# A second pair of projection tiles by Strassen's method in 5 of 11 iterations of a feed-forward layer

## The reference

```
h = x @ w_up + b_up                      # 512 x 1024 times 1024 x 5632
h = causal_depthwise_conv(h, w_dw, b_dw) # width 3
g, val = split(h)                        # 2816 channels each
y = (silu(g) * val) @ w_down + b_down
x = layer_norm(alpha * x + y)
```

## Time and profile before

| | before |
|---|---|
| median of 3 runs | 1030.0 us |
| span of the profiled execution | 1027.8 us |
| what lies around the span, taken against the median | 2.2 us |
| DVE, ACT, POOL busy, share of the span | 78%, 49%, 22% |
| mean granted clock of TensorE | 0.998 of full |

### The profile page before, as it was taken

The page is one execution under the profiler, slowest core; times in us unless marked ns, Lnnn a source line. Parts: engine busy times, 40 slices in busy tenths (PEclk is TensorE's granted clock), DMA queues, the critical chain, the costliest instruction groups (busy, mean ns, idle before and its releaser), DMA issues.

```text
span 1027.8 us, 14241 instructions
## 1 busy us (share of the span) xinstructions
PE 1016.9 (99%) x4731; PEld 842.4 (82%) x4731; DVE 806.6 (78%) x1156; ACT 504.1 (49%) x739; POOL 224.6 (22%) x279
## 2 busy tenths in 40 slices
PE   9999999999999999999999999999999999999997
PEld 7777787988888888888888888898888888888885
DVE  6999978687767767787895869768777776778888
ACT  6889864333334334465454443344343343346553
POOL 1998730413440000000010200052334000000001
PEclk9999999999999999999999999999999999999999
DMA  9756269899995232376655333879999523228652
GB/s 335 217 159 164 62 151 347 177 265 290 228 259 143 102 102 82 118 271 204 195 175 201 118 111 112 308 154 284 270 235 248 148 82 105 99 88 264 201 197 111
DMA packets 64428, 189.71 MB, mean 185 GB/s; under 512 B 7424, under 2 KB 8448, under 8 KB 63872
## 3 DMA queue, kind: packets, MB, share of 16 engines
q1 hardware_dynamic: 44144, 137.76, 39.4%
q0 software_dynamic: 18224, 44.05, 21.7%
q10 hardware_dynamic: 2016, 7.34, 2.0%
HBM read 178.11 MB, written 54.53 MB: 226 GB/s over the span
## 4 chain that ended last, share of the span: by engine, by line
PE 84%; DVE 3%; issue 1%; DMA 1%; ACT 1%; POOL 0%; DVEq 0%; POOLq 0%; ACTq 0%
PE ps L1671 17%; PE ps L1669 17%; PE ps L1670 17%; PE ps L1908 6%; PE ps L1907 6%; PE ps L1906 6%; PE ps L1679 4%; PE ps L1681 4%; PE ps L1680 4%; PE ps L1836 1%; DMA raw<-d_weights 1%; DVE ps L1173 1%; PE ps L1951 1%; PE ps L1953 1%; PE ps L1952 1%
## 5 line engine op out<-in xcount | busy, mean ns | idle before, releaser
L1669 PE MATMUL ps<-xh,wh 128*128 128x512 f32 x816 | 320.3, 392 | 0.4 <-DVE wl L1077 0.3
L1671 PE MATMUL ps<-xh,wl 128*128 128x512 f32 x816 | 317.6, 389 | 0.0
L1670 PE MATMUL ps<-xl,wh 128*128 128x512 f32 x816 | 317.5, 389 | 0.0
L1669 PEld LDWEIGHTS ps<-xh,wh 128*128 128x128 f32 x816 | 153.2, 188 | 33.6 <-issue 1.2
L1670 PEld LDWEIGHTS ps<-xl,wh 128*128 128x128 f32 x816 | 153.2, 188 | 32.8 <-issue 1.2
L1671 PEld LDWEIGHTS ps<-xh,wl 128*128 128x128 f32 x816 | 153.2, 188 | 32.1
L687 ACT ACTIVATE wh<-raw 128x1024 fp32r<-128x1024 f32 x114 | 119.9, 1056 | 81.4 <-PE ps L1908 63.3
L1077 DVE TENSOR_TENSOR wl<-raw,wh 128x1024 fp32r<-128x1024 f32 x101 | 122.6, 1220 | 41.7 <-ACT wh L687 39.9
L536 POOL TENSOR_SCALAR veps<-sqs 128x1 f32<-128x1 f32 x15 | 4.8, 323 | 561.5 <-ACT squares L881 561.5
L1402 DVE TENSOR_TENSOR wl<-raw,wh 128x1024 fp32r<-128x1024 f32 x80 | 97.6, 1220 | 7.6 <-ACT wh L935 7.6
L1906 PE MATMUL ps<-wh,parts 128*128 128x512 f32 x264 | 102.7, 389 | 0.0
(11 more groups left out here) (199 smaller groups left out, 1657.7 us busy)
## 6 DMA issues: line engine op xcount, KB each, us to landing
raw<-d_weights SPq DMA_DIRECT2D x156, 512.0 KB, 4.0
raw<-summed SPq DMA_DIRECT2D x56, 512.0 KB, 4.1
summed<-d_weights POOLq DMA_DIRECT2D x88, 256.0 KB, 8.1
summed<-d_weights SPq DMA_DIRECT2D x66, 256.0 KB, 7.5
summed<-summed POOLq DMA_DIRECT2D x46, 256.0 KB, 5.0
wl<-raw POOLq DMA_DIRECT2D x4, 1024.0 KB, 7.2
wl<-raw POOLq DMA_DIRECT2D x5, 512.0 KB, 7.3
xraw<-d_x_fm SPq DMA_DIRECT2D x8, 256.0 KB, 6.1
```

Source lines behind the costliest of these rows:

```text
L1669: eng.matmul(ps[:, bank, cols], a, xh[:, k, cols], start=(k == 0), stop=False)
L1670: eng.matmul(ps[:, bank, cols], a, xl[:, k, cols], start=False, stop=False)
L1671: mm = eng.matmul(ps[:, bank, cols], b, xh[:, k, cols], start=False, stop=(k == KD - 1))
```

## The change

Iterations 2 to 6 of 11 treat their second tile (units c = 2 and 3) otherwise. The 256 x 1024 weights (gate and value, each as two halves of 4 blocks) and x (two halves of channels, two halves of 256 positions) are taken as 2 x 2 blocks, and the product is made of 7 products of 12 matmuls with 256 columns in place of 8 blocks' worth (48 matmuls of 512 columns).

- The four sums of x are made once per layer by POOL (`x_sums`, 10 operations of 1024 elements per partition), ahead of its DMA steps. ACT and DVE split them (`t_h`, `t_l`, 4 of 1024 each) between iterations 1 and 2.
- The four sums of weights are made per iteration by POOL in the raw buffers (`w_sums`, 4 operations of 512 elements), once the low part of v2 is made. Between them POOL issues its DMA steps: 5 before the first set, 8 behind each.
- ACT and DVE split the sums; DVE adds bias, product and a copy that ACT took of the PSUM bank (`kept`, `block`, 256 columns each, 4 an iteration).
- SP loads into the raw buffers of such a pair only after the low parts of the sums.
- In all iterations the first tap is done by ACT, a second pass over the bank with the tap's weight as scale and a bias that POOL computes once (`tapb`); DVE does two taps.
- PE waits, ahead of a unit, for ACT's reads (`g_in`, `v_in`) in place of the first tap.
- Buffers for the early units, the norm's scratch and one wait (unit U_UP1 - 1, now for the last spatial product) are moved to make room.

The diff, cut to its core:

```diff
+S_FROM, S_TO = 2, 7
+NS = S_TO - S_FROM
+T_ROWS = slice(S_TO, S_TO + 4)
+POOL_STEPS = [5, 8, 8, 8, 8, 8]
...
         elif u == BEFORE_EARLY[1]:
-            eng.wait_ge(v_n, NT)
+            eng.wait_ge(sp, GROUPS)
...
         for u in range(2 * RAW, UNITS):
             eng.wait_ge(*lo_of(u - RAW))
+            if strassen_pair(u - RAW):
+                m, c = strassen_pair(u - RAW)
+                eng.wait_ge(s_lo, 3 * m + (3 if c == 2 else 2))
...
+        eng.tensor_tensor(tapb[:, :], par[:, C_FUP_B:C_FUP_B + n], newest, ALU.mult).then_inc(tapb_ok, 1)
+        eng.wait_ge(tapb_ok, 1)
+        eng.tensor_tensor(tapb[:, :], tapb[:, :], par[:, C_FDW_B:C_FDW_B + n], ALU.add).then_inc(tapb_ok, 1)
...
+        def x_sums(layer):
+
+            eng.wait_ge(x_lo, XN[2 * layer])
...
+            eng.tensor_tensor(t_f[0], b12[0], b11[0], ALU.subtract).then_inc(t_sum, 1)
+            eng.tensor_tensor(t_part[0], b12[1], b11[1], ALU.subtract).then_inc(t_sum, 1)
+            eng.wait_ge(t_sum, n + 2)
+            eng.tensor_tensor(t_f[0], t_f[0], t_part[0], ALU.add).then_inc(t_sum, 1)
...
+        def w_sums(layer, m):
...
+            eng.wait_ge(*lo_of(u + 1))
+            eng.tensor_tensor(a22, a21, a22, ALU.add).then_inc(s_sum, 1)
+            eng.wait_ge(s_sum, n + 1)
+            eng.tensor_tensor(a21, a11, a21, ALU.subtract).then_inc(s_sum, 1)
+            eng.wait_ge(s_sum, n + 2)
+            eng.tensor_tensor(a11, a22, a11, ALU.subtract).then_inc(s_sum, 1)
+            eng.wait_ge(s_sum, n + 3)
+            eng.tensor_tensor(a12, a12, a11, ALU.subtract).then_inc(s_sum, 1)
+
+        def up_sums(layer):
+
+            x_sums(layer)
+            done = POOL_STEPS[0]
+            summed_weights(layer, 0, done)
+            for m in range(NS):
+                w_sums(layer, m)
+                summed_weights(layer, done, done + POOL_STEPS[m + 1])
+                done += POOL_STEPS[m + 1]
+            summed_weights(layer, done, 5 * KQ)
```

ScalarE, the Strassen iteration and the order of the iterations:

```diff
+            def started(i, q, v):
...
+                eng.activation(buf[:, FPAD:], bank, ACT.Identity, bias=par[:, bass.ds(column(i, q, v) + C_FUP_B, 1)])
+                if v == 0:
+                    products_read(i, q)
+                eng.activation(acc[:, :], bank, ACT.Identity, scale=par[:, bass.ds(newest_at(i, q, v), 1)],
+                               bias=tapb[:, bass.ds(column(i, q, v), 1)]).then_inc(signal, 1)
...
+            def strassen(i):
+
+                eng.wait_ge(w_used, i * 4 + u0)
+                eng.wait_ge(raw_in[raw3], i * 16 + loads_of(raw3) + 16 * ((u0 + 3) // RAW))
+                eng.activation(v2h[:, :], raw[:, raw3, HALF:UNIT], ACT.Copy).then_inc(w_hi, 1)
+                started(i, 0, 0)
+                ahead(i, 1)
+                eng.wait_ge(s_sum, i * 4 + (4 * m0 + 2))
+                eng.activation(wh[:, three, :], raw[:, raw3, :], ACT.Copy).then_inc(s_hi, 1)
+                eng.wait_ge(s_sum, i * 4 + (4 * m0 + 3))
+                eng.activation(sum2h[:, :], raw[:, raw2, 0:HALF], ACT.Copy).then_inc(s_hi, 1)
+                started(i, 0, 1)
+                eng.wait_ge(st_pe, i * 5 + (5 * m0 + 1))
+                kept(i, 0, 0, x_bank)
+                eng.wait_ge(s_sum, i * 4 + (4 * m0 + 4))
+                eng.activation(wh[:, two, 0:HALF], raw[:, raw2, HALF:UNIT], ACT.Copy).then_inc(s_hi, 1)
+                gate(i, 0)
+                ahead(i, 2)
+                eng.wait_ge(st_pe, i * 5 + (5 * m0 + 3))
+                kept(i, 1, 1, y_bank)
+                high(i, 0)
+                eng.wait_ge(st_pe, i * 5 + (5 * m0 + 4))
+                kept(i, 0, 1, x_bank)
+                eng.wait_ge(st_pe, i * 5 + (5 * m0 + 5))
+                kept(i, 1, 0, z_second)
+                ahead(i, 3)
+                products_read(i, 1)
...
+                gate(i, 1)
+                high(i, 1)
+
+            regular(0, lambda c: his([u0 + c + LEAD] if c else []))
+            with eng.Fori(1, S_FROM) as i:
+                regular(i, lambda c: ahead(i, c))
+            for j in (0, 1, 3, 2):
+                eng.wait_ge(t_sum, T_SUMS * layer + T_ENDS[j])
+                eng.activation(t_h[j], t_f[j], ACT.Copy).then_inc(t_hi, 1)
+            eng.wait_ge(res_ok, NT * (2 * layer + 1))
+            with eng.Fori(S_FROM, S_TO) as i:
+                strassen(i)
+            with eng.Fori(S_TO, KQ) as i:
+                regular(i, lambda c: ahead(i, c))
```

VectorE:

```diff
+            def strassen(i):
+
+                eng.wait_ge(w_hi, i * 4 + (u0 + 4))
+                eng.tensor_tensor(v2l[:, :], raw[:, raw3, HALF:UNIT], v2h[:, :].bitcast(f32), ALU.subtract).then_inc(w_lo, 1)
+                taps(i, 0, 0)
+                ahead(i, 1)
+                eng.wait_ge(s_hi, i * 3 + (3 * m0 + 1))
+                eng.tensor_tensor(wl[:, three, :], raw[:, raw3, :], wh[:, three, :].bitcast(f32), ALU.subtract).then_inc(s_lo, 1)
+                eng.wait_ge(s_hi, i * 3 + (3 * m0 + 2))
+                eng.tensor_tensor(sum2l[:, :], raw[:, raw2, 0:HALF], sum2h[:, :].bitcast(f32), ALU.subtract).then_inc(s_lo, 1)
+                taps(i, 0, 1)
+                eng.wait_ge(s_hi, i * 3 + (3 * m0 + 3))
+                eng.tensor_tensor(wl[:, two, 0:HALF], raw[:, raw2, HALF:UNIT], wh[:, two, 0:HALF].bitcast(f32), ALU.subtract).then_inc(s_lo, 1)
+                hidden(i, 0)
+                ahead(i, 2)
...
+                block(i, 0, 0, z_first)
...
+                block(i, 0, 1, y_bank)
+                ahead(i, 3)
...
+                block(i, 1, 1, x_bank)
+                block(i, 1, 0, x_bank)
+                taps(i, 1, 0)
+                taps(i, 1, 1)
+                hidden(i, 1)
...
+            for n, j in enumerate((0, 1, 3, 2)):
+                eng.wait_ge(t_hi, 4 * layer + n + 1)
+                eng.tensor_tensor(t_l[j], t_f[j], t_h[j].bitcast(f32), ALU.subtract).then_inc(t_lo, 1)
+            with eng.Fori(S_FROM, S_TO) as i:
+                strassen(i)
```

TensorE:

```diff
+            def strassen_units(i):
+
+                eng.wait_ge(w_lo, i * 4 + (u_up + 3 - len(BY_DMA)))
+                eng.wait_ge(v_in, i * 2 + KH * layer)
+                part(x_bank, wh[:, two, first], wl[:, two, first], b11, True).then_inc(st_pe, 1)
+                part(z_first, wh[:, two, second], wl[:, two, second], b21, True).then_inc(st_pe, 1)
+                eng.wait_ge(s_lo, i * 3 + (3 * m0 + 1))
+                part(y_bank, wh[:, three, second], wl[:, three, second], b_t[0], True).then_inc(st_pe, 1)
+                eng.wait_ge(s_lo, i * 3 + (3 * m0 + 2))
+                eng.wait_ge(snap, i * 4 + (4 * m0 + 1))
+                part(x_bank, sum2h, sum2l, b_t[1], False).then_inc(st_pe, 1)
+                eng.wait_ge(w_lo, i * 4 + (u_up + 4 - len(BY_DMA)))
+                part(z_second, v2h, v2l, b_t[3], True).then_inc(st_pe, 1)
+                eng.wait_ge(s_lo, i * 3 + (3 * m0 + 3))
+                eng.wait_ge(snap, i * 4 + (4 * m0 + 2))
+                part(y_bank, wh[:, two, first], wl[:, two, first], b22, False).then_inc(w_used, 1)
+                eng.wait_ge(snap, i * 4 + (4 * m0 + 3))
+                part(x_bank, wh[:, three, first], wl[:, three, first], b_t[2], False).then_inc(w_used, 1)
+
+            with eng.Fori(1, S_FROM) as i:
                 for c in range(4):
...
+                    regular_unit(i, c)
+            eng.wait_ge(t_lo, 4 * (layer + 1))
+            with eng.Fori(S_FROM, S_TO) as i:
+                for c in range(2):
+                    regular_unit(i, c)
+                strassen_units(i)
+            with eng.Fori(S_TO, KQ) as i:
+                for c in range(4):
+                    regular_unit(i, c)
```

More of the change, by code:

```diff
@@ L630, in issue @@
                     eng.dma_start(out, of).then_inc(w_sum[i % AHEAD], 16)
[L632 removed]
+            for step in range(first_step, last_step):
+                phase, i = divmod(step, KQ)
                 turn(i)
[L634 to L639 removed]
@@ new lines, in ffn_up, with ahead @@
+            other = 4 - bank0
+            x_bank, y_bank = ps[:, bank0 + 3, 0:HQ], ps[:, bank0 + 2, 0:HQ]
+            z_second = ps[:, other + 1, 0:HQ]
+            two, three = [(slot0 + c) % RING for c in (2, 3)]
+            raw2, raw3 = [(u0 + c) % RAW for c in (2, 3)]
+            m0 = layer * NS - S_FROM
+            pads = ((gpad, gacc, g_in), (vpad, vacc, v_in))
+            def ahead(i, c):
+                slot, part = (slot0 + c + LEAD) % RING, (u0 + c + LEAD) % RAW
+                eng.wait_ge(w_used, i * 4 + (u0 + c + LEAD - RING + 1))
+                eng.wait_ge(raw_in[part], i * 16 + loads_of(part) + 16 * ((u0 + c + LEAD) // RAW))
+                eng.activation(wh[:, slot, :], raw[:, part, :], ACT.Copy).then_inc(w_hi, 1)
@@ L930, in ffn_up, with regular @@
[L930 to L937 removed]
+            def regular(i, split):
+                for q in range(2):
+                    split(2 * q)
+                    started(i, q, 0)
+                    split(2 * q + 1)
+                    started(i, q, 1)
+                    gate(i, q)
```

(1 more changed line is left out.)

292 lines of the change are left out of this document (193 added, 99 removed).

## The result

The changed kernel takes 1123.9 us (median of 4 runs, 1122.0 to 1125.5) against 1030.3 for the kernel before in the same session: ratio 1.0917, 95% interval 1.0903 to 1.0930. The forecast was 1113, range 1065 to 1145. The profiled execution, the shortest of the four (1122.0), has a span of 1120.2, 92.4 more than the 1027.8 of before.

The account below looks back on a forecast made before the run. It took TensorE, busy 99% of a 1027.8 us span, as the bound. Per layer -4.0 + 25.5 + 2 + 18.2 = +41.7; two layers +83.4; 1027.8 + 83.4 + 2.2 = 1113 us, range 1065 to 1145.

Parts of the forecast that it names:

- the three places it named: PE idle in iteration 1 (late low weight part), before iteration 2 (11 us), and at product 3 of iterations 3 to 6.
- Term 1: Strassen's products on PE: 84 matmuls of 256 columns replace 48 of 512, saving 0.80 us a pair, 8.0 in all.
- Term 2: PE's wait for the splits of the input sums, in iteration 1 and before iteration 2: 25.5 us lost per layer.
- 197.7 + 37.2 + 20: Time of the input sums' last low part: first taps' start, VectorE's work, eight remaining GpSimd sums; together 254.9 us.
- The floor of 10.8: Least idle PE per layer before iteration 2, 10.8 us, from splitting the input sums if nothing else is late.
- Term 3: PE's clock falls when idle; restart at half speed after the 11 us wait costs 2 us per layer, between 0 and 4.
- The second rival: More than counted: half-clock matmuls after each 4.4 us wait, late GpSimd DMA steps; 1135 to 1160, chance 0.12 above 1145.
- Term 4: PE waits inside Strassen iterations for low parts of weight sums: 3.2 us in the second, 5.0 in three others, 18.2 per layer.
- Edits at nothing: GpSimd's DMA steps, ScalarE's first tap, the later unit wait cost nothing; the small tap-bias operations at most 1.5 us once.
- They just fit: GpSimd's eight DMA steps, 21 us, plus 5.6 of sums fit the about 28 us between first and second sets of sums.
- POOL's sums run beside DVE: GpSimd's sums overlap VectorE or find its gaps: 1060, half exclusion some 1085; chance 0.22 for 1055 to 1085.
- Faster: PE's wait for input-sum splits passes during earlier matmuls, weight sums' low parts come by 13.8: 1022 us, chance 0.02.

Follow-up runs that it names:

- e11: Changed kernel with Strassen in iterations 3 to 6 only, all sums by VectorE, splits reordered, PE's wait inside, product 5 before 3 and 4: 1030.2 us, ratio 1.0016.
- e3: Changed kernel with the ten sums of inputs moved from GpSimd to VectorE, behind its last low part of x: 1108.6 us.
- e4: Changed kernel with GpSimd's DMA steps per iteration 11, 0, 8, 8, 9, 9 instead of 5, 8, 8, 8, 8, 8: 1115.3 us.
- e2: Changed kernel without Strassen: all iterations regular, no sums, first tap still on ScalarE: 1029.4 us against 1029.5 for the kernel before, ratio 0.9997.
- e8: Changed kernel with PE's wait inside, splits earlier, sums of inputs by VectorE, and the sums of weights by VectorE too: 1057.7 us.

## Why the prediction held, and where it didn't

The direction and the main mechanism held: the forecast's own case (1085 to 1145) came true, with PE idle at the three places it named. The sum, 1113, is 10.9 under the measured 1123.9, and two errors of opposite sign are in it: idle 87.4 forecast, 77.0 measured (-10.4); clock 4 forecast, 23.1 measured (+19). That it came within 1% is partly luck. (The two errors make 9 of the 10.9; the profiled execution took 1122.0.)

- **Term 1, products, -8.0**: held (20.92 us an iteration in e11). The gap of the Trainium skill, by which it would have been 11.9, did not; the section gives that formula for a matmul by itself and not for a stream with weight loads, as this one is.
- **Term 2, 25.5 of idle a layer**: 19.1 (7.33 + 11.75). The step that failed is the sum "197.7 + 37.2 + 20": it put GpSimd's time and VectorE's end to end, as if each operation kept the other engine out for its whole length. VectorE did wait like that, but GpSimd's ten sums took 27.0 for 24.4, so of VectorE's 6.5 us of own work in that stretch only 2.6 came on top and 3.9 lay inside GpSimd's. That is the size of the miss: by the prediction's own numbers iteration 2 starts 254.9 - 229.2 = 25.7 late (it says 25.5), and it started some 21.5 late, of which 19.1 is idle and 2.5 the slow matmuls behind the first wait. The floor of 10.8 was close (11.75, and 12.9 in e3, where nothing of GpSimd's stood in the way).
- **Term 3, clock, +2 a layer**: some 12 (23.1 in the two). This is the most mis-sized term. It counted one restart a layer; there are five, since the wait in iteration 1 and those inside the iterations are followed by a lower clock too. The size of one restart, 1.4 to 2.7, is close to the 2 assumed. (The 18 transposes at the start stand 0.213 apart, not 0.228, and the same shape stands 0.108 apart later, at full clock, so the reading as the low level is borne out.) The second rival had this price ("each wait of 4.4 us costs half-clock matmuls", 1.3 to 2 us in six iterations); it belonged in the sum.
- **Term 4, 18.2 a layer**: 20.1 and 18.5, so the number held and its working did only in part. It gave 3.2 and three times 5.0; measured were 7.6, 2.6, 6.5, 3.4. The chain alone makes product 3 wait 2.5 (e4, iteration 3), where the forecast had 4.4 at product 3 and 5.0 in all. In that iteration v2's low part was done 8.2 us behind the previous iteration's last product, for the 10.2 of the forecast, and GpSimd's first two sums took 3.0 for 4.2; the two low parts behind them took 5.0 for 3.7. What was missing is that a raw load doesn't always land in 4.0: its median was 5.2, and the one that set iteration 3's wait took 9.7, issued at 267.11 behind twelve of GpSimd's transfers, eight of them still under way. So the number of this term is near by luck: the chain was counted too long and the load too short. "They just fit", said of GpSimd's eight DMA steps, held for GpSimd (it was waiting for VectorE before each set of sums) and missed what the steps do to SP's load.
- **Edits at nothing**: held for the first tap on ScalarE and the moved buffers (e2 gives 0.9997). GpSimd's DMA steps were not nothing, see term 4.
- **Rivals**: of "POOL's sums run beside DVE" the half is true, seen from GpSimd. "Faster" asked for under 4 us of waits a layer for 5 pairs. e11 had 2.8 a layer, under the 3.2 that its 4 pairs a layer save, and still took 1.2 us more than the kernel before: the rest of 2.1 in the account is not in that condition. 3 of its 5.5 us of waits are the price of VectorE's sums at the start.

The prediction weighed a rule of the Trainium skill (SBUF — State Buffer, SBUF: two separate sides), by which the engine that comes second fully blocks for the whole of the other's instruction. It agrees with what VectorE does here: beside GpSimd's sums its 0.75 became 1.5 to 2.9 and its 1.22 became 2.3 to 3.4, until GpSimd's operation was over. It fits GpSimd less well in these traces: beside VectorE a sum of 2.40 became 2.72 to 3.25, 0.3 longer for a tap of 0.75 and 0.85 for a low part of 1.22.

Not settled: what e11's remaining 2 us of rest are (not a lower clock: in the two up projections its trace shows no stretch under full); why some waits of 2.5 us are followed by slow matmuls and others not; how e8's gain divides; and whether the sums of inputs could be spread over iterations 0 and 1 at no cost, which was not tried.

## What to carry to other kernels

A saving on the bound engine is only worth its own size (here 0.8 us of 21.8) if the work it hands to the others stays off that engine's path. Count the chain from the last thing the bound engine gives to the first it takes, with the landing time of the load at its worst and not at its median. Here, work put on GpSimd beside a VectorE that is busy 77% of the span was paid by VectorE; the same four operations on VectorE itself were cheaper, the freer transfers included. And when a split waits for a late load, look first at what is queued behind it: moving it back gave 13.8 us without making any load faster.
